# Neighbourhood attention: the values of the item two steps back move to the head of the step, and VectorE multiplies them out in that same step

## What is computed

```python
sc = jnp.einsum('bjqhd,bkjchd->bhjqkc', qb, k_band).astype(jnp.float32) * scale
bias = rpb_col[:, row_idx].transpose(0, 2, 3, 1, 4)
sc = jnp.where(mask, sc + bias.astype(jnp.float32), -jnp.inf)
p = jax.nn.softmax(sc, axis=(-2, -1)).astype(v.dtype)
o = jnp.einsum('bhjqkc,bkjchd->bjqhd', p, v_band)
...
o_b = o_b * jax.nn.silu(g_b)
mixed = jnp.concatenate([o_a, o_b], axis=-1)
x = x + mixed @ w_out[l]
```

## Time and profile before

| | before |
|---|---|
| median of 3 runs | 1838.8 us (1837.65 to 1839.38) |
| the profiled execution | 1836.31 us, span 1834.5 us |
| PE busy | 1787.0 us, 97% of the span |
| DVE busy | 912.9 us, 50% |
| ACT busy | 826.7 us, 45% |
| POOL busy | 443.8 us, 24% |
| chain that ended last | PE 89%, ACT 5%, DVE 3% |
| mean granted clock of PE | 0.997 |

### The profile page before, as it was taken

One profiled execution on the slowest core, in us unless ns is written; L12 is line 12 of the kernel. 1 busy time (PEld: TensorE's weight loads), 2 busy tenths in 40 slices (PEclk: granted clock), 3 DMA queues, 4 the chain that ended last, 5 costly groups with the idle time before them and its releaser, 6 DMA issues.

```text
span 1834.5 us, 39079 instructions
## 1 busy us (share of the span) xinstructions
PE 1787.0 (97%) x16429; PEld 1425.6 (78%) x16429; DVE 912.9 (50%) x1992; ACT 826.7 (45%) x1798; POOL 443.8 (24%) x459
## 2 busy tenths in 40 slices
PE   9999999999999999999999999999999999999998
PEld 8997766788887789876776777777777886668887
DVE  5667766333533546024454554555544157775513
ACT  5346666333543534234444444444443256655421
POOL 5650000111111441223232333232323201002221
PEclk9999999999999999999999999999999999999999
DMA  5143310233334232332212222222223220005432
GB/s 195 48 168 94 89 44 1 93 97 118 99 98 141 94 126 84 107 100 79 65 62 62 74 65 63 70 65 65 67 74 102 87 89 13 1 1 195 154 146 92
DMA packets 146007, 159.93 MB, mean 87 GB/s; under 512 B 15092, under 2 KB 123960, under 8 KB 145832
## 3 DMA queue, kind: packets, MB, share of 16 engines
q1 hardware_dynamic: 145800, 157.37, 26.8%
q0 software_dynamic: 32, 0.07, 0.0%
HBM read 110.53 MB, written 52.62 MB: 89 GB/s over the span
## 4 chain that ended last, share of the span: by engine, by line
PE 89%; ACT 5%; DVE 3%; issue 1%; POOL 1%; DMA 1%; DVEq 0%; POOLq 0%; ACTq 0%; SPq 0%
PE ps L1003 9%; PE ps L701 7%; PE ps L1004 7%; PE ps L1005 7%; PE ps L702 7%; PE ps L703 7%; PE ps L1132 4%; PE ps L816 3%; PE ps L795 3%; PE ps L895 3%; PE ps L896 3%; PE ps L897 3%; PE ps L803 3%; PE ps L1321 3%; PE ps L1344 2%; PE ps L1331 2%
## 5 line engine op out<-in xcount | busy, mean ns | idle before, releaser
L2846 POOL TENSOR_TENSOR t<-t,t 128x512 fp32r<-128x512 f32 x183 | 239.5, 1321 | 794.6 <-ACT t L1448 773.7
L1003 PE MATMUL ps<-t,t 128*128 128x512 f32 (+2 forms) x720 | 291.9, 405 | 1.5 <-POOL t L2846 1.5
L701 PE MATMUL ps<-t,t 128*128 128x256 f32 (+2 forms) x872 | 282.2, 324 | 1.7 <-ACT t L1455 1.0
L702 PE MATMUL ps<-t,t 128*128 128x256 f32 (+2 forms) x872 | 276.4, 317 | 0.0
L703 PE MATMUL ps<-t,t 128*128 128x256 f32 (+2 forms) x872 | 276.4, 317 | 0.0
L1005 PE MATMUL ps<-t,t 128*128 128x512 f32 (+2 forms) x720 | 268.4, 373 | 0.0
L1004 PE MATMUL ps<-t,t 128*128 128x512 f32 (+2 forms) x720 | 268.3, 373 | 0.0
L701 PEld LDWEIGHTS ps<-t,t 128*128 128x128 f32 x872 | 165.7, 190 | 18.3 <-issue 6.9
L703 PEld LDWEIGHTS ps<-t,t 128*128 128x128 f32 x872 | 165.7, 190 | 10.4
L702 PEld LDWEIGHTS ps<-t,t 128*128 128x128 f32 x872 | 165.9, 190 | 10.2 <-issue 0.4
L1003 PEld LDWEIGHTS ps<-t,t 128*128 128x128 f32 x720 | 135.8, 189 | 37.4 <-issue 14.7
(11 more groups left out here) (272 smaller groups left out, 3237.2 us busy)
## 6 DMA issues: line engine op xcount, KB each, us to landing
t<-in_w_in SPq DMA_DIRECT2D x53, 512.0 KB, 5.8
zgate_spill<-t SPq DMA_DIRECT2D x20, 512.0 KB, 3.2
tile_bias<-t SPq DMA_DIRECT2D x16, 576.0 KB
t<-tile_bias SPq DMA_DIRECT2D x8, 1152.0 KB, 5.9
t<-zgate_spill SPq DMA_DIRECT2D x16, 512.0 KB, 4.0
feat_spill<-t SPq DMA_DIRECT2D x13, 512.0 KB, 3.3
tile_bias<-band_bias SPq DMA_DIRECT2D x48, 128.0 KB
t<-values_and_gates SPq DMA_DIRECT2D x96, 64.0 KB
```

The lines of the kernel that those rows point to most:

```text
L701: e.matmul(dst, lh, rh, start=k == 0, stop=False)
L702: e.matmul(dst, lh, rl, start=False, stop=False)
L1003: e.matmul(dst, lh, rh, start=k == 0, stop=False)
L2846: e.tensor_tensor(WLO[wslot(b)][:, o], WST[:, o], WHI[wslot(b)][:, o].bitcast(F), ALU.subtract).then_inc(w_lo.sem, w_lo.up((b, p)))
```

## The change

In each step, PE and ACT do the value of m-2 first, ahead of scores and turn; DVE's output in a step is that of m-2, the item whose values PE has just started, where it was that of m-3. In the loop over `QK`, DVE has two outputs left to do where there were three, and the output of item 93 (`B_Z + 29`) is no longer needed after the last step, since step 7 does it.

```diff
@@ pe_program
                 for n in range(8):
                     m = B_Z + 8 * p + n
+                    if n > 1:
+                        band_value(m - 2)
                     band_scores(m)
...
                     if n:
                         band_turn(m - 1)
-                    if n > 1:
-                        band_value(m - 2)
@@ dve_program
                 for x, (what, half) in enumerate(QK):
-                    if p and x < 3:
-                        band_output(B_Z + 8 * p - 3 + x)
+                    if p and x < 2:
+                        band_output(B_Z + 8 * p - 2 + x)
                         if x == 0:
                             band_gates(B_Z + 8 * p - 1)
@@
-                    if n > 2:
-                        band_output(m - 3)
+                    if n > 1:
+                        band_output(m - 2)
@@
-            band_output(B_Z + 29)
             band_part(3, 0)
```

## The result

The changed kernel takes **1843.64 us** (median of 7 runs, 1842.08 to 1847.77), the kernel before beside it 1837.65 (7 runs, 1835.43 to 1839.38): a ratio of 1.0038, 95% interval 1.0028 to 1.0047, 6.0 us slower. The forecast was 1843.0, in a range from 1839.0 to 1848.5. The seven runs lie in two groups, four from 1842.1 to 1843.6 and three from 1847.4 to 1847.8; the mean granted clock was 0.995 or 0.996 in the four and 0.992 in the three. The profiled execution is of the second, 1847.77 us with a span of 1846.0.

A forecast was written before the change was run, and what follows sets the result against it. The prediction took TensorE to bound pairs 0 to 2 and DVE to be tighter in the last pair. Its terms, -2.7 - 0.7 + 7.6 = +4.2 us, moved the median from 1838.8 to 1843.0 us, range 1839.0 to 1848.5.

The forecast's parts named there:

- Two regimes, two signs: Neighbourhood attention: pairs 0 to 2, paced by TensorE, gain 2.7 us; the last pair, where DVE is tighter, loses 7.6.
- Pairs 0 to 2, -2.7 us: Steps 2 to 7 of three pairs: PE's new block order saves 0.15 us in each of 18 steps; bounds 0 and -3.4.
- the 0.09: Pairs 0 to 2: possible extra saving per step, as scores follow dense matmuls after 0.21 us against a spacing of 0.12.
- The rival by which order costs nothing: PE's block order in pairs 0 to 2 gains nothing, leaving +7.6 and -0.7: 1845.7 us; chance 0.15.
- The cover of 0.9 us: Pairs 0 to 2: DVE's gates are done at +4.5 us and PE wants them at +5.4, so the new wait costs nothing.
- Between pairs, -0.7 us: Before the last pair, PE's 0.69 us stall ahead of line 879 vanishes; loss bound +0.5 us.
- they land some 1.8 us earlier: Weights before the last pair arrive sooner because the gate loads, a fifth of the traffic, start after them; 1.1 would suffice.
- The late loads of SP: Between pairs, SP's loads queued behind the late gates pass on 2 us, 7 before the last pair; priced at nothing.
- The circle, 4.60 us a step: Last pair: DVE's rows and gates, PE's value and scores, and back to DVE form a closed chain of 4.60 us.
- The 0.05 from the gates to line 879: Last pair: the time from the end of DVE's gates to PE's value, counted as 0.05 us of the 4.60.
- The last pair, +7.6: The output product starts 7.6 us later, with the clock restored after one step; bounds +6.5 and up to 5.8 more.
- the low clock through the last pair: Rival: the clock stays at 1.2 GHz, five further steps cost 1.16 us more each, 5.8 in all: 1848.8 us; chance 0.10.

The follow-up runs named there:

- first_pairs: The change kept in pairs 0 to 2 and undone in the last pair's steps; 1835.19 us against 1837.03 for the kernel before, ratio 0.999.
- last_pair: The change in the last pair alone, pairs 0 to 2 and the loop between them as before; 1844.78 us, ratio 1.0044 to the kernel before.
- dve_old: The changed kernel with DVE put back in its order of before, PE and ACT as changed; 1866.47 us, ratio 1.0156 to the kernel before.
- filled: The changed kernel plus unused matmuls on constant data ahead of each value in the last pair; 1844.26 us, ratio 1.0037 to the kernel before.
- firsts_late: first_pairs with DVE's six copies moved behind the last pair's steps and POOL's eight subtractions ahead of its six; 1833.4 us, ratio 0.9977.
- gates_first: first_pairs with the old pair's last gates ahead of DVE's output between pairs; one run 1834.3 us, the same kernel timed as gates_first_5 1833.93 us, ratio 0.998.

## Why the prediction was right

- **Two regimes, two signs.** Right, and shown apart: first_pairs gains 1.8 us by the medians and 3.9 by its stage, last_pair loses 7.8 by both. What was not in the prediction: in the last pair PE's part and DVE's part each close a circle without the other.
- **Pairs 0 to 2, -2.7 us: mis-sized.** It measured -3.4 by the steps (with the boundary -3.6, in first_pairs -3.9), its own bound. I took the mean of 0.10 and 0.19 per step because I doubted that the switch into the scores could be saved; the step of 5.33 us is exactly the sum with the 0.09 saved. The rival by which order costs nothing falls. It had leaned on the partial reorder window of the Trainium skill (TensorE: Matmul & The Clock Gate, "Architectural detail"); whatever that window pulls ahead, here the same blocks in another order took 5.33 us where they had taken 5.52, in every one of the 18 steps and in each kernel that has both halves there.
- **The cover of 0.9 us there held.** In the changed kernel no value waits in those pairs. What I did not ask is what DVE's own move does for them: dve_old shows that without it these pairs take 18.5 us more than with it.
- **Between pairs, -0.7 us: mis-sized.** About -0.2 in the profiled execution of the change; the stall was 0.53 us there, 0.75 in filled and 0.27 in first_pairs, which have the same loop between the pairs. The step that failed is "they land some 1.8 us earlier": the share of the bytes is not the share of the time. The weights landed 0.7 us earlier, under the 1.1 that were needed, and over ten profiles the gate loads' share is some 0.5. The late loads of SP cost nothing, as said.
- **The circle, 4.60 us a step.** Measured 4.62 and 4.63 in last_pair and 4.60 to 4.62 in the steps at full clock of the change. That close a fit is in part luck. The 0.05 from the gates to line 879 was no wait for DVE: in the row it came from PE had been busy with the turn until that moment. The real step is 0.15 (609.15 after 608.71 + 0.29, both in last_pair), and the gates' row, taken beside a POOL instruction, had been 0.05 too long, the two lines of the value 0.04. **The last pair, +7.6:** +7.8 in last_pair, where the clock comes back after one step. The price of a step at the low clock was set at 1.16 us more; the one step that lies wholly in it took 5.97, 1.35 more.
- **The clock.** I set the low clock through the last pair against the forecast, 0.10 to 0.60. It was neither: one profiled execution of the change lost it again in alternate steps and after the last one, 4.6 us more, and two other runs of the seven have its time and its mean clock. The argument that failed is that "PE kept the full clock at 340 us through a stretch with idle gaps too": one stretch that kept it does not show that the next will. The prediction had each step from the second on either at full or at half clock; it had no case for a clock that changes from step to step.
- **The total.** Forecast +4.2, measured +6.0. By the stages the gains were 3.4 + 0.2 where 2.7 + 0.7 stood, the last pair 7.8 where 7.6 stood: together +4.2. The rest, 1.8, is not tied to any stage. The clock is the likely place: three of seven runs are slow by it, which makes the median the slowest of the other four, whose own median is 1842.2, 4.6 above; and there are falls in the second block, two in the change's profiled execution and one before. How many of those each timed run had is open, since only profiled executions show them. That the forecast of 1843.0 lies 0.6 us from the measured 1843.64 is luck in part: the difference was 1.8 too small, and the kernel before measured 1.15 less beside the change than the 1838.8 that the forecast started from.

Also open: why the clock falls behind a given wait in one execution and not in another, and how much of what firsts_late gains on DVE is fewer instructions and how much POOL out of its way. A version with the change's order and DVE's copies removed was not tried.

## What to carry to other kernels

Price a change of order once for each regime that it passes through: 0.19 us gained in 18 steps was worth less than the 7.8 us lost in the six of the last pair. Before an engine's own instruction moves ahead of the next item, follow its inputs back; if they come from that engine's last step through another engine, the overlap becomes a circle, and the sum of its rows is the length of a step. Where a stage leaves the matrix engine gaps, look at the granted clock behind them, and read a term of a few us from its stage, not from the total.

## What the runs showed of the hardware

- At one place of the program the clock fell from 2.4 to 1.2 GHz in one execution and not in another, of the same kernel (gates_first and gates_first_5, granted clock 0.79 against 1.00 from 1315 to 1323 us), and behind another wait in first_pairs and not in the kernel before (0.79 against 1.00 from 994 to 1002 us). It was low for some 3.4 us, which cost about 1.6. Fifteen added matmuls in two steps removed one stretch at 1.2 GHz, and with it 2.1 us of the last pair (26.6 against 24.5).
- Two of DVE's instructions, the gates and the copy, end only after the POOL instruction that runs beside them. In the kernel before, DVE's gates at 596.71 took 1.39 us, without POOL 0.29 (at 601.72), and the copy behind them 1.49, elsewhere 0.42. POOL's row there, then DVE's copy:

```profile
596.67 1.28 POOL L2943 TENSOR_TENSOR t<-t,t 128x512 fp32r<-128x512 f32 x1
```

```profile
598.02 1.49 DVE L2264 CAST t<-t 128x512 fp32r<-128x512 f32 x1
```

  The gates end at 598.10, 0.15 us after POOL's instruction (597.95). In firsts_late they end at 593.08, again 0.15 after POOL's instruction (591.65 + 1.28). DVE's other work is not held up: the bias sum at 595.40, which reads PSUM, and the maximum at 595.98, with a single input, took their usual 0.55 us beside POOL's instruction of 595.44 to 596.72. The Trainium skill (SBUF — State Buffer, "SBUF: two separate sides") says that the two engines share a pair of ports under an exclusive lock, held for a whole instruction, and that DVE needs it for an instruction in a two-port mode or with two inputs in SBUF. The gates have two inputs in SBUF, and this case agrees, by both times. I had read the 1.39 us and priced it as fixed.
- Half a megabyte in small loads beside a load of one megabyte delayed it by some 0.5 us (means of five profiles each, 8.8 against 8.3 us; single ones overlap), under a third of the 1.8 that their share of the bytes would give.
